# A four-stage transformer kernel on one core: feed-forward first chunks in more PSUM banks, the first one's tail rewoven, the hybrid's scan moved and its PA bank read out in two halves

## The reference

```python
x = x + gla_mixer(rmsnorm(x, mix_norm_w), ...)            # stage 1
x = x + conv_ffn(rmsnorm(x, ffn_norm_w), ...)             # stage 2
x = rmsnorm(x, final_norm_w)
x = x + hybrid_mixer(rms_norm(x, norm_mix), ...)          # stage 3
x = x + square(relu(rms_norm(x, norm_mlp) @ w_up)) @ w_down   # stage 4
x = rms_norm(x, norm_final)

def conv_ffn(h, w_up, conv_w, conv_b, w_down):            # causal convolution of 3 taps
    u = causal_dwconv(h @ w_up, conv_w, conv_b)
    g, val = split(u, 2);  return (silu(g) * val) @ w_down

def hybrid_mixer(h, ...):
    xa, ga, q, f, v, g, m_a, m_b = split(h @ w_in, ...)
    y_a = rg_lru(causal_conv(xa)) * gelu(ga)              # a gated linear recurrence, a scan over the sequence
    y_b = rms_norm(hgrn2(silu(q), f, v)) * silu(g)        # linear attention with decay, 8 heads
    return (sigmoid(m_a) * y_a + sigmoid(m_b) * y_b) @ w_out
```

## Time and profile before

| | |
|---|---|
| median of 3 runs | 2982.33 us (2978.79 to 2984.19) |
| the profiled execution | 2984.49 us, span in the trace 2982.7 us |
| mean granted clock of PE | 0.966 of full speed |
| PE busy | 2813.7 us, 94% |
| PEld, DVE, ACT, POOL busy | 2325.7, 1545.7, 1042.7, 1619.8 us |

### The profile page before, as it was taken

The page is one execution under the profiler, slowest core; times in us unless marked ns, Lnnn a source line. Parts: engine busy times, 40 slices in busy tenths (PEclk is TensorE's granted clock), DMA queues, the critical chain, the costliest instruction groups (busy, mean ns, idle before and its releaser), DMA issues. The chain is left out here.

```text
span 2982.7 us, 38829 instructions
## 1 busy us (share of the span) xinstructions
PE 2813.7 (94%) x13679; PEld 2325.7 (78%) x13679; DVE 1545.7 (52%) x1973; ACT 1042.7 (35%) x1484; POOL 1619.8 (54%) x1096
## 2 busy tenths in 40 slices
PE   7999997899999999589999999999998999999998
PEld 6888785688888887477787787777777788888886
DVE  3324425355646465846566566566444444444455
ACT  3312315332333232434444444443524222222222
POOL 3332334677777775664465465465433656555552
PEclk8999998999999999799999999999999999999999
DMA  3111110112121212111121121121250111111112
GB/s 116 36 43 35 42 35 1 50 43 63 42 63 42 63 42 71 60 46 47 43 61 45 45 60 32 57 60 33 83 185 8 50 49 56 56 56 43 48 49 84
DMA packets 200710, 160.09 MB, mean 54 GB/s; under 512 B 6231, under 2 KB 176812, under 8 KB 200621
## 3 DMA queue, kind: packets, MB, share of 16 engines
q1 hardware_dynamic: 200621, 158.83, 17.6%
HBM read 143.08 MB, written 15.73 MB: 53 GB/s over the span
## 5 line engine op out<-in xcount | busy, mean ns | idle before, releaser
L313 POOL TENSOR_TENSOR w_lo<-w_raw,w_hi 128x512 fp32r<-128x512 f32 x280 | 397.7, 1427 | 306.8 <-ACT w_hi L307 306.5
L409 PE MATMUL PA<-h_hi,w_hi 128*128 128x512 f32 x840 | 352.7, 420 | 60.7 <-ACT hy_gm L2342 20.9
L410 PE MATMUL PA<-h_lo,w_hi 128*128 128x512 f32 x840 | 340.4, 405 | 0.0
L411 PE MATMUL PA<-h_hi,w_lo 128*128 128x512 f32 x840 | 339.3, 404 | 0.0
L313 POOL TENSOR_TENSOR w_lo<-f_sums,w_hi 128x512 fp32r<-128x512 f32 x114 | 168.1, 1475 | 169.2 <-ACT w_hi L307 169.2
L307 ACT CAST w_hi<-w_raw 128x512 fp32r<-128x512 f32 x280 | 168.6, 616 | 244.7 <-DMA w_raw<-in_w_in 116.1
L409 PEld LDWEIGHTS PA<-h_hi,w_hi 128*128 128x128 f32 x840 | 166.0, 198 | 103.0 <-issue 34.4
L409 PE MATMUL PB<-f_t_hi,w_hi 128*128 128x512 f32 x560 | 221.0, 395 | 1.8 <-ACT hy_tm L2345 0.9
L411 PE MATMUL PB<-f_t_hi,w_lo 128*128 128x512 f32 x560 | 218.3, 390 | 0.0
L410 PE MATMUL PB<-f_t_lo,w_hi 128*128 128x512 f32 x560 | 217.9, 389 | 0.0
L313 POOL TENSOR_TENSOR w_lo<-w_lo_raw,w_hi 128x512 fp32r<-128x512 f32 x108 | 140.2, 1304 | 131.6 <-ACT w_hi L307 131.6
(11 more groups left out here) (472 smaller groups left out, 7137.9 us busy)
## 6 DMA issues: line engine op xcount, KB each, us to landing
w_raw<-in_w_in SPq DMA_DIRECT2D x64, 512.0 KB, 5.3
w_raw<-in_ffn_w_up SPq DMA_DIRECT2D x44, 512.0 KB, 4.5
w_raw<-in_w_up SPq DMA_DIRECT2D x32, 512.0 KB, 5.3
w_lo_raw<-in_w_down SPq DMA_DIRECT2D x64, 256.0 KB, 2.6
w_raw<-in_gla_w_in SPq DMA_DIRECT2D x24, 512.0 KB, 3.7
w_lo_raw<-in_ffn_w_down SPq DMA_DIRECT2D x44, 256.0 KB, 2.6
X<-in_x SPq DMA_DIRECT2D x8, 512.0 KB, 7.7
w_raw<-in_gla_w_out SPq DMA_DIRECT2D x8, 512.0 KB, 3.6
```

What stands on the lines that cost most here:

```text
L313: pool.tensor_tensor(lo, source, hi.bitcast(F32), ALU.subtract).then_inc(self.split, 1)
L409: pe.matmul(bank, ah[:, k, :], bh[:, k, :], start=(k == 0 and not more), stop=False, skip_group_check=more)
L410: pe.matmul(bank, ah[:, k, :], bl[:, k, :], start=False, stop=False, skip_group_check=more)
L411: mm = pe.matmul(bank, al[:, k, :], bh[:, k, :], start=False, stop=(k == 3), skip_group_check=more)
```

## The change

- **First chunks of the feed-forwards.** Unit 1 of chunk 0 (`gated_ffn`) and chunk 0's only unit (`square_ffn`) go to DD and MM, which are free then (`pair_of`). Their successors no longer wait for DVE's reads of PA. The second unit to be loaded gets raw buffers of its own (`give_second`), filled at the stage's start. ACT makes more high parts ahead of `shift` (the first read of PA and PB). Chunk 1 is taken out of the loops.
- **End of `gated_ffn`.** The last chunk's tiles use DD alone; MM holds the norm's row, copied there by ACT, and the scaling (now L717) reads X and MM. The residual's multiplication is gone: X is stored after POOL's `weigh`, and the hybrid applies the factor (`r1`) where it adds its output to x. The rounds' arrivals, turns and low parts are interleaved otherwise, the second half's down weights are cast before the activation's second part, and the square root's table is loaded early.
- **Hybrid.** The 31 small instructions of `tables` move behind the fourth product of xa. PA is read in two halves: the left half after P2 (semaphore `x1`), the right half after c12. P1 of the next unit waits for `x1`, and P5 and P7 for the rest. lruC0 moves behind gm0's last combination. Spare buffers change, and so what "keep" waits for. In FINAL the output weights W1 come before B0, and two of them (W2) behind Y^.
- **`square_ffn`'s end.** The last chunk's activations get buffers of their own (those of h), their parts are made in the middle of the last additions, and the ring's slots shift by one, so that the last down weights need not wait. The norm's row is loaded late.

```diff
@@ pair_product, and gated_ffn
+            def pair_of(i, u):
+                return (c.DD, c.MM) if isinstance(i, int) and i == 0 and u == 1 else (c.PA, c.PB)
-                    gate = {"P1": (s["conv"], j * 2 - 1), "P7": (s["conv"], j * 2), "P2": (s["kept"], j + 1),
+                    free = j - 1 if isinstance(i, int) and j in (1, 2) else j
+                    gate = {"P1": (s["conv"], free * 2 - 1), "P7": (s["conv"], free * 2), "P2": (s["kept"], j + 1),
...
-                up(0, 1)
-                with sp.Fori(1, chunks) as i:
+                ring.load_second(sp, tiles_of(0, 1))
+                up(1, 0, up_at(0, 1) - 1)
+                down(1, 0)
+                up(1, 1)
+                down(1, 1)
+                with sp.Fori(2, chunks) as i:
@@ DoubleNorm
-                dve.scalar_tensor_tensor(out=self.x(k).rearrange("p (b s) -> p b s", s=P),
-                                         in0=c.X[:, self.ORDER[k], :].rearrange("p (b s) -> p b s", s=P),
-                                         scalar=c.rs[:, k:k + 1], in1=self.rows[1], op0=ALU.mult, op1=ALU.mult).then_inc(done, 1)
+            dve.scalar_tensor_tensor(out=self.x(k), in0=c.X[:, self.ORDER[k], :], scalar=c.rs[:, k:k + 1],
+                                     in1=c.MM, op0=ALU.mult, op1=ALU.mult).then_inc(done, 1)
...
-            if -1 <= q < 3:
-                for h in range(2):
-                    x = c.X[:, self.ORDER[2 * q + 2 + h], :]
-                    dve.tensor_scalar(x, x, self.inverses[:, q + 1, h:h + 1], None, ALU.mult).then_inc(self.residual, 1)
@@ DoubleNorm.store
-            sp.wait_ge(self.residual, k + 1)
+            sp.wait_ge(self.weighed, k + 1)
@@ hybrid, the table
-                 "gm0.1 VT0 L2/0 gm0.2 lruD0 gm0.3 L3/0 gm0.4 lruB0 gm0.5 L4/0 lruC0 gm0.6 gm0.7 gm0 VT1 L5/0 "
+                 "gm0.1 VT0 L2/0 gm0.2 lruD0 gm0.3 L3/0 gm0.4 lruB0 gm0.5 L4/0 gm0.6 gm0.7 gm0 lruC0 VT1 L5/0 "
...
-        FINAL = ("U0 gb1^ L5^ W0 gbd1^ A0 L6^ A1 A2 KT^ A3 O0^ A4 O1^ A5 O2^ A6 O3^ XA B0 SQ^ B1 B2 OT^ B3 Y^ B4 W1 B5 B6 "
-                 "XB").split()
+        FINAL = ("U0 gb1^ L5^ W0 gbd1^ A0 L6^ A1 A2 KT^ A3 O0^ A4 O1^ A5 O2^ A6 O3^ XA W1 B0 SQ^ B1 B2 OT^ B3 Y^ W2 B4 "
+                 "B5 B6 XB").split()
@@ hybrid, PE
-                        if nth in (1, 3):
-                            by, per, more = TAKEN[name][nth // 2]
+                        if nth == 1:
+                            wait(pe, s["x1"], u)
+                        elif nth in (2, 3):
+                            by, per, more = TAKEN[name][nth - 2]
@@ hybrid, ACT
+                    def first_pair(out, *args):
+                        k = PRODUCED.index(x)
+                        act.wait_ge(ring.used, ring.done(i, 7 * k + PRODUCTS.index("P2")))
+                        act.activation(out[:, 0:HALF], X1, *args).then_inc(s["x1"], 1)
+                        act.wait_ge(s["c12"], i * 8 + k + 1)
+                        return act.activation(out[:, HALF:SEQ], W1, *args)
...
-                        act.activation(GM, c.PA, ACT.Gelu_apprx_tanh).then_inc(s["ga"], 1)
+                        first_pair(GM, ACT.Gelu_apprx_tanh).then_inc(s["ga"], 1)
@@ hybrid, keep on ACT
-                                "gm0": (s["o_mm"], 2 * i * MT), "gb0": (s["vt_mm"], 2 * i + 2),
+                                "gm0": (s["o_mm"], 2 * i * MT), "gb0": (s["h"], 2 * i + 1),
...
-                                "gb1": (s["y_hi_out"], 32 * i + 16)}[name])
+                                "gb1": (s["lru_m"], 2 * i + 2)}[name])
@@ hybrid, DVE
+                        if isinstance(i, int) and x == "xa.4":
+                            tables()
@@ square_ffn, Ring
+        ring.final = chunks
-        n = self.number(self.place(i, p)[0])
+        n = (self.number(self.place(i, p)[0]) - self.at_end(i)) % SLOTS
```

More of the change, by code:

```diff
@@ L1840, in _, with chunk @@
                 prod(0, 1)
[L1841 to L1842 removed]
+                def chunk(i):
                     combine(i)
```

426 lines of the change are left out of this document (269 added, 157 removed).

## The result

The changed kernel takes 2907.47 us (median of 4, 2904.09 to 2911.14) against 2980.8 us (median of 4) for the one before: a ratio of 0.9753, with a 95% interval of 0.9736 to 0.977. That is 73 us less; the forecast was 95 less, 2890 us, with a range of 2874 to 2918.

What follows compares the result with a forecast made beforehand. PE, busy 2813.7 of 2982.7 us, was taken as the bound, so only its idle time and the clock lost behind waits could be won. Terms summed to 95.0 off 2984.5, giving a forecast of 2890 us, range 2874 to 2918.

Steps and rivals of the forecast that it cites:

- Start of `gated_ffn`: Waits of 4.71 and 7.65 us go, with clock, less 0.6: −16.6 us; −18.6 counting the first tile 2 us earlier.
- End of `gated_ffn`: Last chunk's tail, bound by VectorE, loses multiplications and cheaper scaling: −18.6 us, or −16.6 without the earlier tile's 2 us.
- with the 14.4 us in which it is idle now that makes 57.8: Tail of `gated_ffn`: VectorE's 43.4 us of remaining work plus its present idle time give the new length, so −21.8.
- the term for MM: Tail of `gated_ffn`: scaling with MM as operand takes 1.28 us instead of 2574 ns, so 10.0 us go.
- Start of the hybrid: From its first product to fq0: moved tables bring ScalarE's chain 6 us earlier, halved readout 2 more: −8.0 us.
- the moved tables now sit before DVE's xa.6, covered by two products: Hybrid's start: the tables behind xa.4 were taken to be hidden by two of PE's products.
- gb0.1: First product of gb0, four times: waits of 16.2 us and 4 × 2.4 of clock go, less new waits: −24.0 us.
- L6/0: Hybrid, behind gb0.2: level the moved scan might delay; 0.45 us allowed per iteration, a rival said 2.5 more (+10).
- Other readouts and loop heads: Hybrid: three waits of 1.54 us and one of 1.0 go, −5.6; half of two loop heads' cost, −3.2.
- The output product and `square_ffn`: Wait for weights' low parts goes, −4.9 us; in `square_ffn` waits at chunk 1, −7.0, and the last chunk, −7.1.
- part of it comes back as new waits: Rival, chance 0.19: half the tail's gain lost (+9.6), L6/0 later (+10), starts 4 less: 2913 us.
- the signs that the prediction named: Right if L717 about 1.3 us, hybrid's first product about 1225, no P1 wait over 1 us, seam clocks above 0.9.

Runs made afterwards that it cites:

- Experiment 10: Changed kernel with unit 1 of `gated_ffn`'s first chunk in PA and PB again, raw buffers and ScalarE's order kept: 2921.61 us.
- Experiment 8: Changed kernel with the tail's rounds reordered (VectorE adds the even tile before the factors, the odd before two low parts): 2914.47 us.
- Experiment 7: Changed kernel with the scaling reading the norm's row from SBUF again instead of from MM: 2908.65 us.
- Experiments 1 to 3: Changed kernel with the tables at the hybrid's start (2909.73 us), all behind xa's last combination c12 (2905.59 us), or in two parts (2900.15 us).
- experiment 3: Changed kernel with 13 table instructions at the hybrid's start and the rest behind xa's last combination c12: 2900.15 us.
- Experiments 4 to 6: Changed kernel with lruC0 back ahead of gm0's last two combinations (2911.33 us), PA read out whole (2919.66 us), or both (2944.51 us).
- experiment 5: Changed kernel with PA read out whole after c12, as before, lruC0 staying where the change put it: 2919.66 us.
- Experiments 11 and 12: Changed kernel with `square_ffn`'s first chunk in PA and PB again (2915.54 us), or without the ring's shift in its last chunk (2913.92 us).

## Why the forecast was right, and what it missed

**Start of `gated_ffn`: right.** −18.1 with the earlier tile against −18.6. The prediction left 0.6 us for a new wait; it was 0.45. Experiment 10 shows that the banks carry 13.5 of it.

**End of `gated_ffn`: right in mechanism, mis-sized.** −11.5 against −16.6. The step that failed is "with the 14.4 us in which it is idle now that makes 57.8", which took VectorE's busy time for the bound and its idle time for fixed. In the 68.2 us VectorE is busy 48.4, not 43.4, and idle 19.7, not 14.4. Most of the 5 us more of work are the factors: their small instructions (L692 to L706) take 11.2 us, where L650 to L663 took 6.6. A round is a chain through four engines: addition, square, weigh on GpSimd (2.4 us), square again, factors, root, scaling. In it stand the factors, whose small instructions take up to 1.27 us beside GpSimd. This chain is read from the rows; no run shortened it. Experiment 8 shows that the order in the round decides: the same instructions in another order took 2 us more. Experiment 7 shows that the term for MM was priced on the old schedule. The rule of the Trainium skill ("SBUF — State Buffer", section "Who interferes with whom") agrees with the row: with one SBUF operand the scaling takes 1277 ns, beside a working GpSimd too. What that is worth here is 2.4 us, not 10.

**Start of the hybrid: wrong.** The chain of weights did move up by 7.4 us, as forecast. The step that failed: "the moved tables now sit before DVE's xa.6, covered by two products". The tables were taken at the 9 us that they had cost in the trace before, where GpSimd happened to be idle for most of the time. At their new place they ran from 1240.37 to 1256.4, 16 us. Two products cover 5.4. At 9 us they would have ended at about 1249.4, and PA's right half would have been free 2.1 us later, about when P1 ends; this is an estimate from the rows, as no run had the tables there at 9 us. Experiments 1 to 3 show that it is the tables that P5 waits for. In the third, 9.7 us come back in this stretch and the whole kernel is 7 us faster, though the small instructions are as dear as before: what helped is that no combination that PE is about to need stands behind them.

That they are dear beside GpSimd fits the rule of the Trainium skill that the prediction quoted for the scaling: two SBUF inputs, and the instruction waits as a whole. The same section ("Who interferes with whom" in "SBUF — State Buffer" of the Trainium skill) says that `tensor_scalar`, too, can enter a mode that takes both port pairs when its operands meet that mode's conditions. The `TENSOR_SCALAR` rows of 1.16 to 1.29 us agree; no row shows the mode itself.

**gb0.1: right in size, wrong in its parts.** The four waits and the clock behind them are gone. The prediction gave the halves the credit and priced the scan's move as a risk only. Experiments 4 to 6 show that each of the two alone suffices, and that without both it is 37 us (33 in the hybrid). L6/0, on which a rival rested, did not become late: of PE's waits for a level the list after has those of 0.57 us per iteration and the 3.05 at head 7, as before, and one new of 0.84 behind the latter.

**Other readouts and loop heads: mostly wrong.** −8.8 was expected. The 1.54 us before gb1.1 became 1.27 before gb1's P7, and the two "issue" waits at the loop heads stayed. The early release of PA helps only up to the readout of PB, which is next; with PA read whole (experiment 5) the wait is before P1 again. Three times 1.27 and the 3.2 us expected of the loop heads make 7, the 6 us that the hybrid's loop lacks against its −25.8.

**The output product and `square_ffn`: right.** −4.8 against −4.9, and −12.4 against −14.1. Experiments 11 and 12 put 8 and 6 us on the two edits in `square_ffn`.

Of the signs that the prediction named, L717 came at 1.28 us and there is no new wait of over 2 us for a level or `kept`. The hybrid's first product came at 1224.42, for "about 1225", but partly by luck: 5.9 us of that are `gla`'s, and the two stretches gave 29.6 us rather than 35.2. Two signs failed: fq0's first product waits 2.79 us, and the clocks at the seams are 0.80 (the tail) and 0.87 (1230 to 1270), not above 0.9. The errors have one sign: no stretch gained clearly more than its forecast, so the total was not brought into its range by errors that cancel.

The rival "part of it comes back as new waits" (2913 us) was nearest, 5.5 us from the measured time, though in other places than it named: neither L6/0 nor the starts of the feed-forwards, but the tables, the tail's rounds and gb1's P7.

Left open: whether the tail's chain could be shortened by having GpSimd's `weigh` elsewhere was not tried. What the 1.65 us of "issue" at the loop heads are is not known either, nor why `gla` varies.

## What to carry to other kernels

A small instruction's price belongs to its place, not to it. If its cheap rows come from a stretch in which the engine that it shares ports with was idle, price it for the new place by rows in which that engine works. Where it can't be made cheap, put it where nothing behind it on its engine is waited for. Two edits that hide the same wait are each worth nothing beside the other: undo them together before calling either useless. And where a tail passes through four engines, look at the chain of one round beside the busiest engine's time. When a stage that nobody touched varies by several us, compare stretches between landmarks before calling an effect of that size a gain or a loss.

## What the runs showed of the hardware

VectorE instructions on 8 or 2 values per partition took 0.17 us beside an idle GpSimd and up to 1.30 us beside a working one, about the length of one of GpSimd's instructions (1.26 to 1.30 us). Beside a `weigh` of 2.4 us one of them (L707 in experiment 8, at 1205.97) took 2.04. In the tail the factors on 2 values (L692) took 1114 ns on average. `RECIPROCAL` did not show it: 0.20 us at 1267.77 in the kernel before and 0.17 at 1194.76 and 1209.03 in the changed one, all beside a working GpSimd. The clock around a wait was as in the earlier trace rows: P5 of fq0, behind its 4.96 us, has steps 1.28 us apart at the end, but the fall to that level came earlier, 1.3 us after the wait of 2.79. In experiment 3, behind a wait of 2.52 us, the window 1230 to 1270 stayed at 0.99. The first 50 us of the program ran at a granted clock of 0.80 in some executions, 0.86 in one, and 0.97 or 1.00 in others, with nothing changed there, and `gla` took 512 to 520 us, a range wider than several of the effects measured here.
